# x loaded first, gate exponentials by polynomial, first expert weights rounded between blocks, and one 512-column tile in each turn of the selection

## The chip, the cores and the metric

The kernel runs on one core of a Trainium2 chip. The metric is the device time of one execution in microseconds (us). The kernel before took 918.75 us, the median of 3 runs (917.81 to 918.88).

## The reference

One layer of a hybrid model: 256 tokens, width 1024, all in float32. Three mixers (a state-space scan, block attention of 8 heads, retention of 4 heads) share one input projection; their outputs are normalised, projected and added to x. Then comes an expert layer, which takes most of the time:

```python
def peer_layer(h, w_q, sub_keys, u_emb, v_emb):
    q = (hf @ w_q).reshape(t, PEER_HEADS, 2, PEER_QDIM // 2)
    sc = jnp.einsum('thcd,hcnd->thcn', q, sub_keys)
    sv, si = lax.top_k(sc, PEER_TOPK)
    cand_s = (sv[:, :, 0, :, None] + sv[:, :, 1, None, :]).reshape(...)
    cand_i = (si[:, :, 0, :, None] * PEER_KEYS + si[:, :, 1, None, :]).reshape(...)
    fs, fp = lax.top_k(cand_s, PEER_TOPK)
    eidx = jnp.take_along_axis(cand_i, fp, axis=-1)
    gates = jax.nn.softmax(fs, axis=-1)
    ...
        act = jax.nn.gelu(jnp.einsum('cd,chkd->chk', xc, u_emb[ic]))
        return jnp.einsum('chk,chkd->cd', gc * act, v_emb[ic])
```

There are 16384 experts. Each token uses 8 x 16 of them.

## The kernel before, in words

**Precision by halves.** Every float32 product of the projections and of the expert layer is made of three matmuls of rounded operands: high x high, high x low, low x high (`halves_product`, lines 439 to 441). ScalarE (ACT) rounds a slice of weights into `w_hi`, GpSimd (POOL) subtracts to give `w_lo`, TensorE (PE) multiplies. For the values the subtraction is VectorE's (DVE).

**The expert layer is dense.** All 16384 experts are multiplied, in 128 tiles of 128 (`NT`), four tiles to a turn (`UN` = 4), 32 turns (`TURNS`). In the first pass (`keys_turn`) a tile of u is multiplied with h for all 256 tokens, passed through Gelu by ACT (line 1603) and kept in memory outside the chip (`spill`). A selection of each token's experts runs beside it on DVE. From turn `G_TURN0` = 15 the selection becomes a dense matrix of gates (`one_hots`, `group_out`). In the second pass (`values_turn`) activations times gates are multiplied with the tiles of v. Tiles of u stand in one of two PSUM banks, 0 or 1, by `s % 2`, so PE starts tile s of a turn only once the Gelu of tile s - 2 is done (`act_ready`, line 727).

**Wide tiles.** A tile whose s is in `wide` is made otherwise (lines 738 to 747): `w_hi` is multiplied in one matmul of 512 columns with `h_both`, the high and the low half of h side by side, so the product with the low half lies in columns 256 to 511 of the bank. ACT copies that part to `low_out` (line 1618, increments `part_ready`), DVE adds it into the first part (`add_part`, increments `added`), and only then does ACT make the Gelu. A tile has then 16 matmuls instead of 24. Before, turns 0, 1, 12, 13 and 14 have three wide tiles each (`WIDE_TURNS`), the turns from 15 on two; turns 2 to 11 have none.

**The order of each engine is written by hand**, and each engine works its list in order. ACT, for each tile of a turn (line 1605 on): the rounding of the next tile in two halves (`high`, lines 1590 to 1597), what is `extra`, the Gelu of a wide tile before this one (it waits for `added`), then the low part's copy or the Gelu of this tile. POOL: two subtractions for each tile (line 1717). The DVE list between the adds of turn 1 and those of turn 12 is the selection: for each half of the tokens (t = 0, 1) `best` over 16 rows of 128 key scores (lines 1185 to 1199: eight best of each row, their indices and a copy without them, the next eight, their indices), sums of pairs in `w2`, `best` over 8 rows of 256 sums, differences to the best one (line 1231), and for both halves of a pair an index look-up by comparison, product and reduction (lines 1240 to 1242). `step` and `settle` wait until DVE's own results are there.

**Gates.** After the selection DVE reports (`diff_ready`), ACT takes the exponentials in turn 13 (`gate_exps`, line 1642), DVE divides by the sums and reports (`tok_ready`, line 1252), and PE transposes the rows before turn 14.

**Queries and the first tile.** The 16 slices of w_q are multiplied in two rounds of 8 (line 690 on): the first round fills banks 4 to 7, the second banks 0 to 3. ACT copies four query banks to `pqT` in `queries(n)` (line 1571). During the second round h is scaled: DVE multiplies into banks 5 to 7, ACT rounds to `h_hi` (line 1583), DVE subtracts to `h_lo`. Then ACT rounds the first expert tile (`high(0, 0, 0)`), runs `queries(1)`, waits for DVE's copy of iota into bank 2 (line 1207) and starts turn 0.

**Beginning and end.** SyncE's queue (SP) issues the loads in this order: parameters, identity, rotations, x in two halves, first weights, constants, and so on (lines 337 to 362). PE is kept at work by 9 matmuls until x is there. At the end DVE adds the four result tiles (two column halves, two token halves) to x; it waits for `half_used`, which counts column halves.

Of the kernel before, what the change touches and what calls it, by code (L numbers as in the profile page):

```python
# [19 lines left out]
F32 = mybir.dt.float32  # L20
F32R = mybir.dt.float32r
U32 = mybir.dt.uint32
ALU = mybir.AluOpType
# [37 lines left out]
OUT_BANKS = ((2, 6), (0, 1))  # L61
ROW_BANKS = (2, 3, 0, 1)
# [11 lines left out]
WIDE_TURNS = {0: 0, 1: 3, EXP_TURN - 1: 6, EXP_TURN: 9, ROUTE_TURN: 12}  # L74
WIDE_S, WIDE_G_S, WIDE_G0 = (0, 1, 2), (0, 2), 15
# [46 lines left out]
def build(nc, x, w_in, vecs, consts, rots, decay, mask, s5_b, s5_c, w_glu, w_out, w_q, keys, u_t, v, out, spill):  # L122
    with ExitStack() as ctx:
# [150 lines left out]
        diff_ready, gate_exp = sem("gate_exponents_ready"), sem("gate_exp_ready")  # L274
# [5 lines left out]
        sum_ready, stored = sem("sum_ready"), sem("stored")  # L280
# [55 lines left out]
        def _(sp):  # L336
            sp.dma_start(vec[:], vecs).then_inc(params_in, 16)
            sp.dma_start(ident, consts[:, C_ID:C_ID + P]).then_inc(con_in, 16)
            sp.dma_start(rawf[:, 256:256 + ROPE_N], rots[:, 0:ROPE_N]).then_inc(rope_in, 16)
# [3 lines left out]
            sp.dma_start(w_ring[0][:, 0:4, 0:S5_CH], first[:, 0:4]).then_inc(first_in, 16)  # L343
            sp.dma_start(times, consts[:, C_IOTA:C_N]).then_inc(times_in, 16)
            sp.dma_start(w_ring[0][:, 4:KC, 0:S5_CH], first[:, 4:KC]).then_inc(w_in_sem[0], 16)
# [63 lines left out]
        def _(pe):  # L409
# [36 lines left out]
            keep_warm(mv[:, 0, 0:P], 7, 9)  # L446
# [241 lines left out]
            for n in range(2):  # L688
                for k in range(KC):
# [6 lines left out]
                    for h in range(4):  # L696
                        c = slice(h * P, (h + 1) * P)
                        mm = halves_product(ps[:, 4 * (1 - n) + h, 0:S],
# [6 lines left out]
                    if n == 1 and k == 2:  # L705
                        pe.wait_ge(rows_ready, 1)
                        pe.wait_ge(pq_ready, 4)
                        for t in range(TT):
                            mm = pe.matmul(ps[:, 4, t * P:(t + 1) * P], rstd_rows[:, t, :], ident, start=True, stop=True)
# [50 lines left out]
            pe.wait_ge(keys_in, 16)  # L760
            key_scores(0)
# [3 lines left out]
            with pe.Fori(2, EXP_TURN - 1) as t:  # L765
                keys_turn(t)
# [16 lines left out]
            def values_turn(t, first=False, last=False):  # L783

                for s in range(UN):
                    pe.wait_ge(w_ready, UN * t + s + 1)
                    for h in range(2):
# [7 lines left out]
                        mm.then_inc(half_used, 1)  # L795
# [8 lines left out]
        def _(dve):  # L804
# [370 lines left out]
            for k in range(KC + 2):  # L1175
                if k >= 2:
                    dve.wait_ge(th_ready, 3 * KC + k - 1)
                    tt(h_lo[:, H2_PLACE[k - 2], :], ps[:, 5 + (k - 2) % 3, 0:S], h_hi[:, H2_PLACE[k - 2], :].bitcast(F32),
                       ALU.subtract).then_inc(tl_ready, 1)
                if k < KC:  # L1180
                    if k >= 3:
                        dve.wait_ge(tl_ready, 3 * KC + k - 2)
                    tt(ps[:, 5 + k % 3, 0:S], hT[:, k, :], ps[:, 4, 0:S], ALU.mult).then_inc(scaled_ready, 1)

            def best(dst, where, src, scratch):
# [604 lines left out]
```

## Time and profile before

| what | value |
|---|---|
| profiled execution, own time | 918.49 us |
| its span, first to last instruction | 916.7 us |
| median of 3 runs | 918.75 us |
| PE busy, share of the span | 903.1 us, 99% |
| DVE, ACT, POOL busy | 713.8, 557.2, 424.9 us |
| mean granted clock of PE | 0.998 of full speed |
| chain that ended last: PE, ACT, DVE, POOL | 93%, 4%, 1%, 1% |
| all waits of PE for POOL's L1717, for ACT's L1603 | 2.5 us (1), 1.4 us (2) |
| ACT table loads | 10, of 1.28 us |

How to read it: PE is busy nearly all the time, and a matmul's record is longer than the distance to the next one (they overlap), so a PE that is busy is not yet one that could not be faster. The distance between the starts of its matmuls tells more. The span is cut in stages: mixers and projections to about 110 us, output projection and queries to 157, turns 0 and 1 to 188.6, turns 2 to 11 with the selection to 303.8, turns 12 to 14 to about 340, the rest of the first pass to about 562, the second pass to 913.

### The profile page before, as it was taken

Reading aid. Unit: us, or ns where it says so; the run is one execution under the profiler, and the core shown is the slowest. Engines: PE = TensorE matmul, PEld = TensorE weight load, DVE = VectorE, ACT = ScalarE, POOL = GpSimd, SP = SyncE. Lnnn points to the kernel's source line nnn. Section 1 sums busy time; section 2 is a strip of 40 time slices with the busy share of each in tenths; the row PEclk is TensorE's granted clock in tenths of the full one; section 3 lists DMA queues with packets and bytes.
Section 4 is the critical chain, followed back from the end, with each engine's and each line's share of the span. In section 5 each row is a group of like instructions: output and inputs, shape, how many; then the busy total and the mean of one; then the engine's idle time right before and its main releaser. Section 6 shows DMA issues by size and latency. Waiting matters only on the chain.

```text
span 916.7 us, 19407 instructions
## 1 busy us (share of the span) xinstructions
PE 903.1 (99%) x5480; PEld 798.9 (87%) x5480; DVE 713.8 (78%) x1604; ACT 557.2 (61%) x1113; POOL 424.9 (46%) x340
## 2 busy tenths in 40 slices
PE   8999998999999999999999999999999999999998
PEld 6877888899999989999999999888888888888886
DVE  6989533099997138898988986888888888888886
ACT  7658565555555666666666666565665656556563
POOL 4874386788888887777777774000000000000000
PEclk9999999999999999999999999999999999999999
DMA  9824050466666666655656566777777677777773
GB/s 327 297 102 181 3 207 1 161 223 224 229 227 228 230 213 205 196 201 187 204 193 197 194 206 210 256 234 242 248 236 245 231 246 244 242 239 233 249 241 124
DMA packets 67756, 191.54 MB, mean 209 GB/s; under 512 B 6672, under 2 KB 8592, under 8 KB 67728
## 3 DMA queue, kind: packets, MB, share of 16 engines
q1 hardware_dynamic: 67728, 191.19, 61.9%
q8 instruction: 15, 0.25, 0.1%
q14 instruction: 13, 0.11, 0.0%
HBM read 173.86 MB, written 17.30 MB: 209 GB/s over the span
## 4 chain that ended last, share of the span: by engine, by line
PE 93%; ACT 4%; DVE 1%; issue 1%; POOL 1%; DMA 0%; SPq 0%; DVEq 0%; POOLq 0%; ACTq 0%
PE ps L439 24%; PE ps L441 24%; PE ps L440 24%; PE ps L744 9%; PE ps L746 4%; PE ps L754 3%; ACT routing L1432 1%; PE ps L743 1%; ACT w_hi L1363 1%; DMA xs<-in_x 0%; POOL w_lo L1702 0%; PE ps L717 0%; PE ps L595 0%; PE ps L431 0%; DVE routing L813 0%
## 5 line engine op out<-in xcount | busy, mean ns | idle before, releaser
L1596 ACT ACTIVATE w_hi<-raw 128x512 fp32r<-128x512 f32 x512 | 308.3, 628 | 134.1 <-PE ps L441 130.4
L1717 POOL TENSOR_TENSOR w_lo<-raw,w_hi 128x512 fp32r<-128x512 f32 x256 | 326.9, 1298 | 80.9 <-ACT w_hi L1596 80.4
L813 DVE TENSOR_TENSOR w_lo<-raw,w_hi 128x512 fp32r<-128x512 f32 x256 | 177.4, 693 | 52.8 <-ACT w_hi L1596 41.4
L439 PE MATMUL ps<-h_both,w_hi 128*128 128x256 f32 x712 | 201.9, 284 | 0.0
L441 PE MATMUL ps<-h_both,w_lo 128*128 128x256 f32 x712 | 201.5, 283 | 0.0
L440 PE MATMUL ps<-h_both,w_hi 128*128 128x256 f32 x712 | 201.4, 283 | 0.0
L439 PE MATMUL ps<-w_hi,hot_gate 128*128 128x512 f32 x512 | 199.2, 389 | 0.0
L440 PE MATMUL ps<-w_lo,hot_gate 128*128 128x512 f32 x512 | 199.2, 389 | 0.0
L441 PE MATMUL ps<-w_hi,hot_gate 128*128 128x512 f32 x512 | 199.2, 389 | 0.0
L744 PE MATMUL ps<-h_both,w_hi 128*128 128x512 f32 x376 | 137.5, 403 | 3.9 <-POOL w_lo L1717 2.5
L439 PEld LDWEIGHTS ps<-h_both,w_hi 128*128 128x128 f32 x712 | 136.0, 191 | 0.4 <-POOL w_lo L1702 0.2
L440 PEld LDWEIGHTS ps<-h_both,w_hi 128*128 128x128 f32 x712 | 136.0, 191 | 0.2
L441 PEld LDWEIGHTS ps<-h_both,w_lo 128*128 128x128 f32 x712 | 136.0, 191 | 0.0
L441 PEld LDWEIGHTS ps<-w_hi,hot_gate 128*128 128x128 f32 x512 | 96.1, 188 | 20.0
L440 PEld LDWEIGHTS ps<-w_lo,hot_gate 128*128 128x128 f32 x512 | 96.1, 188 | 20.0
L439 PEld LDWEIGHTS ps<-w_hi,hot_gate 128*128 128x128 f32 x512 | 96.1, 188 | 19.8
L1702 POOL TENSOR_TENSOR w_lo<-routing,w_hi 128x512 fp32r<-128x512 f32 x72 | 92.3, 1299 | 45.2 <-ACT w_hi L1363 43.6
L1603 ACT ACTIVATE acts<-ps 128x256 f32<-128x256 f32 x128 | 49.1, 383 | 100.8 <-PE ps L441 93.7
L1281 DVE SCALAR_TENSOR_TENSOR hot_gate<-ps,route_t 128x256 fp32r<-128x256 f32 x256 | 105.7, 476 | 0.0
L746 PE MATMUL ps<-h_both,w_lo 128*128 128x256 f32 x329 | 93.0, 283 | 0.0
L744 PEld LDWEIGHTS ps<-h_both,w_hi 128*128 128x128 f32 x376 | 70.9, 190 | 18.1 <-ACT routing L1574 2.7
L813 DVE TENSOR_TENSOR route_t<-acts,routing 128x256 f32<-128x256 f32 x128 | 81.7, 638 | 4.3 <-ACT acts L1603 2.1
(222 smaller groups left out, 1109.7 us busy)
## 6 DMA issues: line engine op xcount, KB each, us to landing
raw<-in_u_t SPq DMA_DIRECT2D x128, 512.0 KB, 3.4
raw<-in_v SPq DMA_DIRECT2D x128, 512.0 KB, 3.3
act_spill<-acts SPq DMA_DIRECT2D x62, 256.0 KB, 2.2
acts<-act_spill SPq DMA_DIRECT2D x62, 256.0 KB, 3.4
routing<-in_w_in SPq DMA_DIRECT2D x4, 2048.0 KB, 12.8
routing<-in_w_out SPq DMA_DIRECT2D x2, 2048.0 KB, 8.2
routing<-in_w_q SPq DMA_DIRECT2D x2, 2048.0 KB, 7.6
routing<-in_w_in SPq DMA_DIRECT2D x2, 1024.0 KB, 9.6
```

Source lines behind the costliest of these rows:

```text
L439: pe.matmul(dst, s_hi, m_hi, start=first and i == 0, stop=False)
L440: pe.matmul(dst, s_hi, m_lo, start=False, stop=False)
L441: mm = pe.matmul(dst, s_lo, m_hi, start=False, stop=end)
L744: mm = pe.matmul(ps[:, s % 2, :], s_hi, both, start=(h == 0 and k == 0), stop=end)
L746: mm = pe.matmul(ps[:, s % 2, 0:S], s_lo, m_hi, start=False, stop=False)
L754: mm = pe.matmul(ps[:, 4 + 2 * (s % 2) + q // 2, (q % 2) * 2 * NKEY:(q % 2 + 1) * 2 * NKEY], hot_j[:, s % 2, q, :], hot_gate[:, s % 2, q]. ...
L813: return V.tensor_tensor(out_, a, b, op)
L1281: ins = V.scalar_tensor_tensor(hot_gate[:, s % 2, q], iota_p.unsqueeze(1).to_broadcast([P, 2, NKEY]), route_t[:, 0, one], route_t[:, 2:4, ...
L1596: A.activation(w_hi[:, 2 * (s % 2) + h, :], raw[:, s, h * HALF:(h + 1) * HALF], ACT.Copy)\
L1603: A.activation(acts[:, s, :], ps[:, s % 2, 0:S], ACT.Gelu_apprx_tanh).then_inc(act_ready, 1)
L1702: G.tensor_tensor(w_lo[:, m % 4, :], w_ring[n % W_SLOTS][:, k, :], w_hi[:, m % 4, :].bitcast(F32), ALU.subtract).then_inc(lo_ready, 1)
L1717: G.tensor_tensor(w_lo[:, slot, :], raw[:, s, h * HALF:(h + 1) * HALF], w_hi[:, slot, :].bitcast(F32), ALU.subtract).then_inc(lo_ready, 1)
```

## The change

It does the following.

- The loads of identity, `vec` and rotations are issued from ACT's queue, in that order, before ACT's first square; SP starts with x, and the second part of the first weights goes ahead of the constants. Seven matmuls instead of nine keep PE at work. On ACT the copies `full(0)` and `full(1)` stand before the first exponential, `full(2)` and `full(3)` before the square root.
- A Gelu of one element is put behind the square root of the third norm.
- The banks of both query rounds, of the rows' transposes, of the output projection's second half and of the scaled h are exchanged (0 to 3 for 4 to 7). The first expert tile's two roundings are put behind blocks 4 and 5 of the scaled h; `queries(1)` is put into tile 0 of turn 0, behind the rounding of tile 1; DVE copies iota as soon as its last `h_lo` is written; PE starts turn 0 when all blocks are scaled.
- In turns 2 to 11 (`WIDE_PICK_S` = (0,), `N_PICK` = 10) the first tile of each turn is wide. DVE makes the ten adds at five places in each half of the selection.
- The gates' exponentials are computed by DVE, by the polynomial of eight terms that the kernel uses for another exponential, and the adds of turn 12 are put between its steps.
- At the end PE reports each of the four result tiles by itself (`out_psum`).

```diff
-OUT_BANKS = ((2, 6), (0, 1))
-ROW_BANKS = (2, 3, 0, 1)
+OUT_BANKS = ((2, 6), (4, 5))
+ROW_BANKS = (6, 7, 4, 5)
...
-WIDE_TURNS = {0: 0, 1: 3, EXP_TURN - 1: 6, EXP_TURN: 9, ROUTE_TURN: 12}
-WIDE_S, WIDE_G_S, WIDE_G0 = (0, 1, 2), (0, 2), 15
+WIDE_PICK_S = (0,)
+N_PICK = EXP_TURN - 3
+WIDE_TURNS = {0: 0, 1: 3, EXP_TURN - 1: 6 + N_PICK, EXP_TURN: 9 + N_PICK, ROUTE_TURN: 12 + N_PICK}
+WIDE_S, WIDE_G_S, WIDE_G0 = (0, 1, 2), (0, 2), 15 + N_PICK
...
         def _(sp):
-            sp.dma_start(vec[:], vecs).then_inc(params_in, 16)
-            sp.dma_start(ident, consts[:, C_ID:C_ID + P]).then_inc(con_in, 16)
-            sp.dma_start(rawf[:, 256:256 + ROPE_N], rots[:, 0:ROPE_N]).then_inc(rope_in, 16)
             for t in range(TT):
...
-            keep_warm(mv[:, 0, 0:P], 7, 9)
+            keep_warm(mv[:, 0, 0:P], 7, 7)
...
             def keys_turn(t, groups=None, first=False, first_group=False, wide=()):
                 for s in range(UN):
-                    if first and s < 2:
-                        pe.wait_ge(pq_ready, 4 + s + 1)
-                    else:
+                    if first and s == 0:
+                        pe.wait_ge(scaled_ready, KC)
+                    elif not (first and s < 2):
                         pe.wait_ge(act_ready, UN * t + s - 1)
...
             with pe.Fori(2, EXP_TURN - 1) as t:
-                keys_turn(t)
+                keys_turn(t, wide=WIDE_PICK_S)
...
+                            if last and s == UN - 1:
+                                mm.then_inc(out_psum, 1)
+                        if not (last and s == UN - 1):
+                            mm.then_inc(half_used, 1)
...
-            dve.wait_ge(pq_ready, PH)
+            dve.wait_ge(tl_ready, 4 * KC)
             V.tensor_copy(iota_p, iota).then_inc(iota_ready, 1)
...
             def best(dst, where, src, scratch, first=None, second=None):
                 for d_, s_ in zip(dst, src):
                     did(V.max(d_[:, 0:8], s_))
                 settle()
+                if first is not None:
+                    add_part(first, 0)
                 for d_, w_, s_, x_ in zip(dst, where, src, scratch):
                     did(V.max_index(w_[:, 0:8], d_[:, 0:8], s_))
                     did(V.match_replace(x_, d_[:, 0:8], s_, LOWEST))
                 settle()
                 for d_, x_ in zip(dst, scratch):
                     did(V.max(d_[:, 8:16], x_))
                 settle()
+                if second is not None:
+                    add_part(second, 0)
...
-                     [sc[:, t, c, h, :] for c, h in ch_rows], [work[:, c, h, :] for c, h in ch_rows])
+                     [sc[:, t, c, h, :] for c, h in ch_rows], [work[:, c, h, :] for c, h in ch_rows], 6 + 5 * t, 7 + 5 * t)
...
-                     [work3[:, h * 256:(h + 1) * 256] for h in range(PH)])
+                     [work3[:, h * 256:(h + 1) * 256] for h in range(PH)], 8 + 5 * t)
+                add_part(9 + 5 * t, 0)
...
                     step(tt(w3, match_p, idx_f[:, c].unsqueeze(2).to_broadcast(shape), ALU.mult))
+                    if c:
+                        add_part(10 + 5 * t, 0)
                     step(V.tensor_reduce(rows[:, t, c, :].rearrange("p (h k) -> p h k", h=PH), w3, AX.X, ALU.add))
-            V.tensor_copy(top2[:, 0, 0:1], top2[:, 0, 1:2]).then_inc(diff_ready, 1)
-            add_parts(EXP_TURN - 1)
-            dve.wait_ge(gate_exp, TT)
...
+            step(V.tensor_scalar(rest_g, gates, -150.0, None, ALU.max))
+            step(V.tensor_scalar(turns_g, rest_g, float(1 / np.log(2)), ROUND, ALU.mult, ALU.add))
+            step(V.tensor_scalar(turns_g, turns_g, -ROUND, None, ALU.add))
+            for ln2_part in (LN2_1, LN2_2):
+                step(V.scalar_tensor_tensor(rest_g, turns_g, -ln2_part, rest_g, ALU.mult, ALU.add))
+            add_part(WIDE_TURNS[EXP_TURN - 1], 0)
+            step(V.tensor_scalar(turns_g, turns_g, -127.0, 127.0, ALU.max, ALU.min))
+            did(V.tensor_scalar(power_g.bitcast(mybir.dt.int32), turns_g, 127.0, float(2 ** 23), ALU.add, ALU.mult))
+            step(V.tensor_scalar(sum_g, rest_g, EXP_C[0], None, ALU.mult))
+            for c_ in EXP_C[1:3]:
+                step(V.scalar_tensor_tensor(sum_g, sum_g, c_, rest_g, ALU.add, ALU.mult))
+            add_part(WIDE_TURNS[EXP_TURN - 1] + 1, 1)
+            for c_ in EXP_C[3:]:
+                step(V.scalar_tensor_tensor(sum_g, sum_g, c_, rest_g, ALU.add, ALU.mult))
+            add_part(WIDE_TURNS[EXP_TURN - 1] + 2, 2)
+            step(V.scalar_tensor_tensor(gates, sum_g, 1.0, power_g, ALU.add, ALU.mult))
...
             for h in range(2):
-                dve.wait_ge(half_used, TAIL + 4 * NT - 1 + h)
                 for t in range(TT):
+                    dve.wait_ge(out_psum, TT * h + t + 1)
...
+            act.dma_start(ident, consts[:, C_ID:C_ID + P]).then_inc(con_in, 16)
+            act.dma_start(vec[:], vecs).then_inc(params_in, 16)
+            act.dma_start(rawf[:, 256:256 + ROPE_N], rots[:, 0:ROPE_N]).then_inc(rope_in, 16)
             squares_x(0)
+            act.wait_ge(params_in, 16)
+            full(0)
+            full(1)
             act.wait_ge(expo_ready, 1)
...
             root(ss_x, 0, 1.0 / D)
+            A.activation(spare, quarter, ACT.Gelu_apprx_tanh)
             slices_high(range(FRONT + 21, FRONT + 3 * KC))
...
+                if k in (4, 5):
+                    high(0, 0, 0, (k - 4,))
...
-            high(0, 0, 0)
-            queries(1)
             act.wait_ge(iota_ready, 1)
-            wide_turn(0, first=True)
+            def last_queries(s):
+                if s == 0:
+                    queries(1)
+
+            wide_turn(0, first=True, extra=last_queries)
...
-            with act.Fori(3, EXP_TURN - 1) as t:
-                keys_turn(t)
+            with act.Fori(3, EXP_TURN - 1) as t:
+                keys_turn(t, wide=WIDE_PICK_S, wide_0=t + 4)
```

## Rows read from the trace of the kernel before

**Rows 1.** Windows: stretch, length, busy time and instructions of each engine, PEclk granted

```profile
160.40:162.50 2.10, 2.10 (x8) 1.80 (x7) 0.00 (x0) 0.69 (x2) 2.00 (x3) 0.51 0.35 84
...
188.60:303.80 115.20, 115.20 (x960) 115.20 (x961) 103.64 (x397) 58.85 (x121) 100.46 (x80) 1.00 0.68 224
```

**Rows 2.** Timeline of PE around turn 0: start, us, [idle before, releaser]

```profile
156.70 0.28 PE L441 MATMUL ps<-h_both,w_lo 128*128 128x256 f32 x1
159.47 0.77 PE L744 MATMUL ps<-h_both,w_hi 128*128 128x512 f32 x1 [2.49 <-POOL w_lo L1717]
...
167.10 0.50 PE L744 MATMUL ps<-h_both,w_hi 128*128 128x512 f32 x1 [0.39 <-ACT acts L1603]
```

**Rows 3.** Timelines of POOL, ACT and DVE around turn 0

```profile
151.05 3.81 POOL L1702 TENSOR_TENSOR w_lo<-routing,w_hi 128x512 fp32r<-128x512 f32 x3 [2.67 <-ACT w_hi L1363]
158.05 5.12 POOL L1717 TENSOR_TENSOR w_lo<-raw,w_hi 128x512 fp32r<-128x512 f32 x4 [3.19 <-ACT w_hi L1596]
...
157.35 1.14 ACT L1596 ACTIVATE w_hi<-raw 128x512 fp32r<-128x512 f32 x2
158.39 1.19 ACT L1574 ACTIVATE routing<-ps 128x256 f32<-128x256 f32 x4
...
165.37 1.28 ACT L1603 ACT_TABLE_LOAD   x1
...
157.49 0.42 DVE L813 TENSOR_TENSOR h_both<-ps,h_both 128x256 fp32r<-128x256 f32 x1 [1.01 <-ACT h_both L1583]
159.62 0.29 DVE L1207 COPY ps<-con 128x128 f32<-128x128 f32 x1 [1.71 <-ACT routing L1574]
```

**Rows 4.** Timelines of ACT, DVE and PE in turns 12 and 13

```profile
306.85 0.39 ACT L1618 ACTIVATE con<-ps 128x256 f32<-128x256 f32 x1 [1.41 <-PE ps L744]
...
309.63 0.38 ACT L1618 ACTIVATE con<-ps 128x256 f32<-128x256 f32 x1 [1.09 <-PE ps L744]
...
307.26 0.43 DVE L813 TENSOR_TENSOR ps<-ps,con 128x256 f32<-128x256 f32 x1 [13.79 <-ACT con L1618]
...
321.04 0.42 DVE L813 TENSOR_TENSOR ps<-ps,con 128x256 f32<-128x256 f32 x1
...
320.50 0.40 PE L744 MATMUL ps<-h_both,w_hi 128*128 128x512 f32 x1
321.93 0.50 PE L744 MATMUL ps<-h_both,w_hi 128*128 128x512 f32 x1 [1.03 <-ACT acts L1603]
```

**Rows 5.** Timelines of POOL and PE in the first query round

```profile
137.03 2.54 POOL L1702 TENSOR_TENSOR w_lo<-routing,w_hi 128x512 fp32r<-128x512 f32 x2 [0.44 <-ACT w_hi L1363]
...
134.41 0.36 PE L439 MATMUL ps<-h_both,w_hi 128*128 128x256 f32 x1
```

**Rows 6.** Timeline of DVE: first instruction behind each place of an add, tokens' first half

```profile
189.00 0.09 DVE L1191 MATCH_VALUE_LOAD routing<-routing 128x8 f32 x1
...
200.71 0.09 DVE L1198 MATCH_VALUE_LOAD routing<-routing 128x8 f32 x1
...
210.91 0.09 DVE L1191 MATCH_VALUE_LOAD routing<-routing 128x8 f32 x1
...
223.40 0.74 DVE L813 TENSOR_TENSOR routing<-routing 128x128 f32<-128x128 f32 x1
...
236.41 2.29 DVE L1242 TENSOR_REDUCE routing<-routing 128x128 f32<-128x2048 f32 x1
```

**Rows 7.** Timeline of DVE: one line of the selection, first and second half

```profile
224.06 0.22 DVE L1234 TENSOR_SCALAR routing<-routing 128x128 uint32<-128x128 uint32 x1
...
277.56 1.31 DVE L1234 TENSOR_SCALAR routing<-routing 128x128 uint32<-128x128 uint32 x1
```

**Rows 8.** Timelines of SP's queue, DVE and PE in the beginning

```profile
2.13 0.91 SPq L341 DMA_DIRECT2D xs<-in_x  x2
...
2.73 0.17 DVE L835 TENSOR_SCALAR small<-vec 128x8 f32<-128x8 f32 x1 [1.70 <-DMA vec<-in_vecs]
...
17.45 0.66 PE L512 MATMUL ps<-con,raw 128*128 128x128 f32 x4 [0.99 <-ACT raw L1464]
```

**Rows 9.** Timeline of DVE at the end

```profile
911.49 2.64 DVE L813 TENSOR_TENSOR xs<-xs,ps 128x512 f32<-128x512 f32 x4 [2.72 <-PE ps L441]
```

More of the change, by code:

```diff
@@ L1182, in _, with add_part, best @@
                         dve.wait_ge(tl_ready, 3 * KC + k - 2)
-                    tt(ps[:, 5 + k % 3, 0:S], hT[:, k, :], ps[:, 4, 0:S], ALU.mult).then_inc(scaled_ready, 1)
-            def best(dst, where, src, scratch):
+                    tt(ps[:, 1 + k % 3, 0:S], hT[:, k, :], ps[:, 0, 0:S], ALU.mult).then_inc(scaled_ready, 1)
+            ch_rows = [(c, h) for c in range(2) for h in range(PH)]
+            shape = [P, PH, PK, PK]
+            w2 = work2.rearrange("p (h a b) -> p h a b", h=PH, a=PK)
+            w3 = work3.rearrange("p (h a b) -> p h a b", h=PH, a=PK)
+            iota_k = iota_p[:, 0:PK].unsqueeze(1).unsqueeze(1).to_broadcast(shape)
+            dve.wait_ge(tl_ready, 4 * KC)
+            V.tensor_copy(iota_p, iota).then_inc(iota_ready, 1)
+            dve.wait_ge(iota_ready, 1)
+            def add_part(n, s):
+                dve.wait_ge(part_ready, n + 1)
+                tt(ps[:, s % 2, 0:S], ps[:, s % 2, 0:S], low_out, ALU.add).then_inc(added, 1)
+            def best(dst, where, src, scratch, first=None, second=None):
                 for d_, s_ in zip(dst, src):
@@ L1247, in _ @@
-            step(V.tensor_reduce(gsum, gates, AX.X, ALU.add))
+            gates = rows[:, :, 2, :]
+            by_t = lambda a: a.rearrange("p (t n) -> p t n", t=TT)
+            rest_g, power_g = by_t(work2[:, 0:2 * P]), by_t(work2[:, 2 * P:4 * P])
+            turns_g, sum_g = by_t(ps[:, 4, 0:2 * P]), by_t(ps[:, 5, 0:2 * P])
+            settle()
+            step(V.tensor_scalar(rest_g, gates, -150.0, None, ALU.max))
+            step(V.tensor_scalar(turns_g, rest_g, float(1 / np.log(2)), ROUND, ALU.mult, ALU.add))
@@ L1446, in _ @@
             squares_x(1)
-            full(0)
-            full(1)
+            full(2)
+            full(3)
             act.wait_ge(zeros_ready, 4)
@@ L1568, in _, with high @@
             root(ss_x, 0, 1.0 / D)
+            A.activation(spare, quarter, ACT.Gelu_apprx_tanh)
             slices_high(range(FRONT + 21, FRONT + 3 * KC))
+            def high(n, s, turn, halves=(0, 1)):
+                act.wait_ge(raw_in[s], 16 * turn + 16)
+                for h in halves:
+                    act.wait_ge(half_used, TAIL + 2 * n + h - 3)
+                    A.activation(w_hi[:, 2 * (s % 2) + h, :], raw[:, s, h * HALF:(h + 1) * HALF], ACT.Copy)\
+                        .then_inc(hi_ready, 1)
             def queries(n):
@@ L1589, in key_scores @@
                              scale=rstd[:, t:t + 1]).then_inc(sc_ready, 1)
-            def high(n, s, turn, halves=(0, 1)):
-                act.wait_ge(raw_in[s], 16 * turn + 16)
-                for h in halves:
-                    act.wait_ge(half_used, TAIL + 2 * n + h - 3)
-                    A.activation(w_hi[:, 2 * (s % 2) + h, :], raw[:, s, h * HALF:(h + 1) * HALF], ACT.Copy)\
-                        .then_inc(hi_ready, 1)
             def gelu(t, s, first):
```

49 lines of the change are left out of this document (16 added, 33 removed).

## The prediction

> **What bounds the kernel now.** I read the busy table first, then the windows, then the timeline of TensorE (PE) wherever its starts are not evenly spaced, then the engine that releases it. In the first turns and the selection PE decides: in the 115.20 us of turns 2 to 11 it issued 960 matmuls without a gap, 0.120 us apart, 24 to a tile, 2.88 us a tile [rows 1]. A change pays there only by fewer PE cycles or by removing a PE wait. The reader should see three such waits. (1) Before the first expert tile: the last query matmul starts at 156.70 and the first expert one at 159.47, released by POOL, and behind it the granted clock is 0.51, the lower level (1.2 GHz), for a stretch [rows 1, 2]. (2) Turn 0, tile 2, at 167.10, behind an ACT table load [rows 2, 3]. (3) Turn 13, tile 2, at 321.93, behind another [rows 4].
>
> **The parts, each priced.** The profiled execution took 918.49 us, 1.79 more than its span of 916.70, and 0.26 less than the median, 918.75. The sum is made against 918.49.
>
> *First expert weights, banks.* Now ACT rounds them at 157.35, after the last of its eight h_hi copies, and POOL's first low half starts at 158.05 although its slices ended at 154.86 (151.05 + 3.81) [rows 3]. After: the two roundings stand behind copies 4 and 5, whose semaphore values they share, so half 0 is rounded by about 153.8 and POOL does its halves at 154.9 and 156.2, 1.27 each. PE starts tile 0 at 156.82, its second half at 158.2; the last low part of h ends at 157.91 (157.49 + 0.42) [rows 3], in time. The wait and the slow clock go. Late next is tile 1: ACT may round it only after the copy of iota, which moves from 159.62 to about 157.97; ACT follows some 0.33 later, POOL 0.70 after ACT starts (157.35 to 158.05) with 1.27, PE 0.15 (159.32 to 159.47 [rows 2]): 160.42, where PE wants it at 156.82 + 2.80 = 159.62. Tile 1 then ends at about 163.3. queries(1), 1.19 of ACT [rows 3], now lies in tile 0, and tile 2's rounding ends at 162.0, its low half at 162.9: covered. The Gelu table (1.28, 165.37 [rows 3]) is loaded early, so tile 2 starts at 163.3 instead of 167.10: **-3.8**. If tile 1 took no wait it would be -4.6; if POOL slipped another tile half, -2.5.
>
> *The early table load* costs ACT about 1.5 in the query stage. POOL's next slice starts at 137.03 and ends 1.3 later; PE's query slices start at 134.41 and last 12 x 0.12 = 1.44, so that slice (the fifth after this start) is wanted at 140.17 [rows 5]. 1.5 later is 139.8: hidden by 0.4, **0**; without this cover up to +1.1.
>
> *Exponentials.* The ACT pair in turn 13 goes. PE's starts were 320.50 and 321.93, 1.43 apart where 0.23 is usual, and the matmuls behind a wait lose 0.1 more [rows 4]: **-1.3**. The 16 polynomial steps of 256 columns are bounded by the 256-column add, 0.43 [rows 4]. They are taken between the adds of turn 12, five at a time: 5 x 0.43 + 0.43 = 2.6 < 2.8. The rest ends soon after turn 12's third tile, and all of turn 13, over 11 us, lies before the route transposes that wait for it: **0**.
>
> *Wide tiles.* ACT's copies of two such tiles are 2.78 apart [rows 4]; I take 2.815, since a tile alone has normal ones on both sides, against 2.88: 10 tiles x 0.065 = **-0.65** (-0.4 to -1.0). The ten extra copies on ACT (0.39 [rows 4]) stand in its idle time before a tile ends.
>
> *What the ten adds wait for* is the new term. Each is written into DVE's selection at a fixed place, five in each half. The part is ready once a turn, every 4 x 2.88 - 0.065 = 11.455. In a turn that goes well DVE's add starts 0.41 behind ACT's copy, and PE's matmul of two tiles on starts 0.89 behind the add [rows 4] (321.93 - 321.04). PE wants that tile 2.88 - 0.21 = 2.67 behind the copy (turn 12 starts at 303.80 [rows 1], its first tile ends 2.82 later and is copied at 306.85, some 0.2 behind); so an add may be 2.67 - 0.41 - 0.89 = 1.37 late for nothing, and beyond it PE waits. DVE's own work between the places, start to start [rows 6]: 11.71 (189.00 to 200.71), 10.20 (to 210.91), 12.49 (to 223.40), 13.01 (to 236.41); then 5.55 in the next half. An add puts 0.34 to it. The first add is on time: DVE is there at 189.00, and turn 2 starts at 188.60 [rows 1], so that its first tile ends at 191.4. Then:
> second add 11.71 + 0.34 - 11.455 = 0.6 late, no wait; third 0.6 + 0.34 + 10.20 - 11.455 < 0, on time; fourth 12.49 + 0.34 - 11.455 = 1.38 late, no wait; fifth 1.38 + 0.34 + 13.01 - 11.455 = 3.27 late.
> To this comes what DVE loses beside POOL: the same 128x128 shift took 0.22 at 224.06 and 1.31 at 277.56 [rows 7], there across one of POOL's 1.27 instructions. With the adds in, the segment begins 2.13 behind a copy, and POOL's pair runs from 0.98 (0.28 for the copy, 0.70) to 3.53, which puts the shift behind its second half as at 277.56: 0.6 more than in the first half of before, 3.9 late. PE waits 3.9 - 1.37 = 2.5, with 0.1 for the restart 2.6. This comes at turn 6, tile 2, and, the second half being alike, at turn 11, tile 2. **+5.2**, bounds 2 x 2.0 = +4.0 (no collision) and 2 x 3.4 = +6.8 (both operations collide). Below: 0, if adds were never late, which needs the 13.01 to shrink by 2.
> The Trainium skill (GPSIMD Engine Reference, Specifications) says that POOL's SBUF interface is shared with VectorE and contended by instructions in a two-port mode or with two SBUF inputs. The trace agrees (1.31 against 0.22). It speaks against the change here, since the added wait makes such steps fall at other moments.
>
> *Start.* x is issued 1.38 earlier (2.13 to 0.75), but vec is now second on ACT's queue and DVE's chain, which starts on it at 2.73, is later by an issue (0.42) or more; PE waits at 17.45 for ACT, where two copies move from behind the second square to before it [rows 8]. No row prices the new order; between -1.4 (the whole shift) and +0.5 (vec's delay on the path), and both ends as near, the middle: **-0.5**. Two warm-up matmuls less: PE waits for x anyway, 0.
>
> *End.* DVE's four last adds, 2.64 together [rows 9], were released by halves; now by tiles of three matmuls, so that one add (0.66) instead of two is left behind the last matmul: **-0.6** (0 to -0.7).
>
> Sum: -3.8 - 1.3 - 0.65 + 5.2 - 0.5 - 0.6 = -1.65, or 918.49 - 1.65 = 916.8; I say **916.9**, 0.20% below the median, on the edge of what a measurement tells from no change (0.2%, 1.8 us, so 916.9 to 920.6 counts as the same).
>
> **Rivals.**
> - *The adds are in time or nearly so.* For: per half DVE has 52.96 + 5 x 0.34 = 54.7 of work for 57.3, so only the places are wrong, not the load; should a step be quicker, the lateness shrinks one for one. Against: the step times above are alike in both halves. No waits: 916.9 - 5.2 = 911.7; one wait of 2.6: 914.3. Chance 0.22.
> - *The clock falls in a wait.* PE idle for 2.49 before 159.47 [rows 2] was followed by a stretch at 0.51, where 8 matmuls took 2.10 [rows 1] and 16 fill 2.8 otherwise. The two new waits are as long. Some 3 us at half speed (159.47 to 162.50) lose about 1.5. One fall 918.4, two 919.9. For: equal idle time. Against: PE was busy right up to both. Chance 0.23. The Trainium skill (TensorE: Matmul & The Clock Gate, Why this matters for your kernels) says to leave no long idle gap between bursts of matmuls, or the engine returns to the lower clock; the row at 0.51 agrees.
> - *The other side: DVE collides with POOL at both steps of the segment and the clock falls each time.* Place: tile 2 of turns 6 and 11. Price: 6.8 instead of 5.2, and 2 x 1.5: 916.9 + 1.6 + 3.0 = 921.5. It decides once the fifth add is over 4.5 late, so that PE idles for over 3. Chance 0.06.
> - *The early rounding does not take effect* (POOL or ACT in another order), and the first wait stays: 916.9 + 3.8 = 920.7. Chance 0.03. Against: the semaphore values are reached in the trace before ACT would ask.
>
> **How the numbers follow.** Forecast 0.46, its own range 915.5 to 918.6 by the collision bounds and the start. Below 916.9 lie half of it (0.24) and the first rival (0.22): faster 0.46. Slower: the third rival and part of the fourth, 0.07. The same: 0.47. For 8 in 10 the range takes in one missing wait and both clock falls: 913.6 to 919.9.
>
> **What would show it.** First expert matmul within 0.3 of the last query one; clock 1.00 there; tile 2 of turn 0 some 3.8 earlier. No table load on ACT between turn 0 and the end. Turns 2 to 11: waits of PE on ACT's Gelu, only in tile 2 of turns 6 and 11, 2.0 to 3.4 each, with the DVE add late behind its copy by as much more than 0.41. If PE waits in other turns, or nowhere, the segment sum is wrong; if the granted clock is below 1.00 after them, the second rival has come. Last DVE adds: one behind the last matmul.

## The result and the profile after

| | kernel before | kernel after |
|---|---|---|
| median | 918.59 us (4 runs) | 926.70 us (4 runs, 925.41 to 928.30) |
| ratio | | 1.0097 (95% interval 1.0085 to 1.0110) |
| profiled execution, span | 918.49, 916.7 us | 928.30, 926.4 us |
| PE's mean granted clock, share of full speed | 0.998 | 0.992 |

The change makes the kernel 8.1 us slower, where 916.9 was forecast. The ratio is not the quotient of the two medians, which is 1.0088. The profiled execution of after is the slowest of its four; the two spans differ by 9.7.

The timeline of after: selected instructions from four stretches, the start, the first expert tile, the selection and the end. Others that lie between them are left out. In brackets stand the idle time ahead and what ended it:

```profile
0.74 0.42 ACTq L1470 DMA_DIRECT2D con<-in_consts  x1
1.19 0.46 ACTq L1471 DMA_DIRECT2D vec<-in_vecs  x1
4.89 1.09 PE L414 MATMUL ps<-con,xs 128*128 128x128 f32 x8 [0.47 <-DMA con<-in_consts]
6.75 0.17 DVE L837 TENSOR_SCALAR small<-vec 128x8 f32<-128x8 f32 x1 [5.72 <-DMA vec<-in_vecs]
9.99 0.21 ACT L1478 ACTIVATE small<-small 128x8 f32<-128x8 f32 x1 [2.05 <-DVE small L815]
10.10 1.04 ACT L1407 ACTIVATE routing<-xs 128x1024 f32<-128x1024 f32 x1
19.56 0.66 PE L510 MATMUL ps<-con,raw 128*128 128x128 f32 x4 [2.35 <-ACT raw L1495]
...
161.14 0.28 PE L439 MATMUL ps<-h_both,w_lo 128*128 128x256 f32 x1
161.26 0.40 PE L742 MATMUL ps<-h_both,w_hi 128*128 128x512 f32 x1
...
228.32 0.43 DVE L815 TENSOR_TENSOR ps<-ps,con 128x256 f32<-128x256 f32 x1
228.87 1.31 DVE L1241 TENSOR_SCALAR routing<-routing 128x128 uint32<-128x128 uint32 x1
230.33 2.59 POOL L1747 TENSOR_TENSOR w_lo<-raw,w_hi 128x512 fp32r<-128x512 f32 x2 [0.24 <-ACT w_hi L1608]
230.35 1.43 DVE L1244 CAST routing<-routing 128x256 f32<-128x256 uint32 x1
238.18 0.38 ACT L1652 ACTIVATE con<-ps 128x256 f32<-128x256 f32 x1 [1.25 <-PE ps L742]
243.44 0.43 DVE L815 TENSOR_TENSOR ps<-ps,con 128x256 f32<-128x256 f32 x1
308.15 0.53 PE L437 MATMUL ps<-h_both,w_hi 128*128 128x256 f32 x1 [3.41 <-ACT acts L1637]
...
921.20 2.73 DVE L815 TENSOR_TENSOR xs<-xs,ps 128x512 f32<-128x512 f32 x4 [2.04 <-PE ps L439]
922.82 0.39 PE L439 MATMUL ps<-w_hi,hot_gate 128*128 128x512 f32 x1
```

Turn 0 went as forecast: the first expert matmul, 161.26, stands 0.12 behind the last query one, where PE had waited 2.49 [rows 2]. The start did not: DVE begins at 6.75 instead of 2.73 and PE at 19.56 instead of 17.45 [rows 8]. In the selection the fifth add of the first half is at 243.44, its copy at 238.18; PE then waits 3.41 in each half (its next matmuls are at 244.42 and 308.15).

The windows of after; the columns are length, PE's busy time (matmuls), its granted clock, DMA share and GB/s:

```profile
19.50:23.00 3.50, 3.14 (x13) 0.79 1.08 376
23.00:27.00 4.00, 4.00 (x19) 0.76 1.03 388
156.00:190.00 34.00, 33.41 (x256) 1.00 0.47 156
244.40:247.80 3.40, 3.38 (x16) 0.50 0.64 196
247.80:251.20 3.40, 3.40 (x21) 0.65 0.61 189
308.10:311.60 3.50, 3.45 (x16) 0.52 0.61 211
311.60:315.00 3.40, 3.40 (x30) 0.99 0.53 169
```

Turn 0 now runs at full clock, against 0.51 in [rows 1]; but the clock falls at three places: in the start, and behind each of the two waits (0.50 is the lower level, 1.2 GHz).

Where the 9.7 us of span came from, by PE's starts in the two profiles (first matmul of the same place, before and after):

| stretch | before | after | difference |
|---|---|---|---|
| up to the transposes of the first normalised rows | 124.20 | 128.36 | +4.16 |
| from there up to the query slice of [rows 5] | 134.41 | 138.84 | +0.27 |
| from there up to turn 2 | 188.49 | 188.98 | -3.94 |
| turns 2 to 11 | 115.33 long | 126.52 long | +11.19 |
| turns 12 and 13, up to the route transposes | 23.91 long | 22.60 long | -1.31 |
| all up to the last matmul | 584.69 long | 584.72 long | 0.0 |
| behind the last matmul | 4.28 long | 3.58 long | -0.7 |

Two rows stand far from their terms: the start (+4.4 against -0.5) and turns 2 to 11 (+11.2 against 5.2 - 0.65 = +4.5).

### The profile page after: what moved, and what is told of

Read it like the earlier page. It is cut to its first block, busy times and chain, and to the rows that moved or that the text cites. A ratio compares the mean times of both kernels' runs of the same rounds, so it can differ in the third digit from the quotient of the medians.

```text
span 926.4 us, 19297 instructions
## 1 busy us (share of the span) xinstructions
PE 906.9 (98%) x5396; PEld 797.9 (86%) x5396; DVE 724.3 (78%) x1629; ACT 554.8 (60%) x1120; POOL 425.6 (46%) x340
## 4 chain that ended last, share of the span: by engine, by line
PE 87%; DVE 7%; ACT 3%; POOL 1%; issue 1%; DMA 1%; ACTq 0%; POOLq 0%; DVEq 0%
PE ps L437 22%; PE ps L439 21%; PE ps L438 21%; PE ps L742 11%; PE ps L744 5%; PE ps L752 3%; DVE ps L815 1%; DVE routing L815 1%; ACT routing L1459 1%; DVE routing L1218 1%; DVE routing L1210 1%; DVE routing L1209 1%; PE ps L741 1%; POOL w_lo L1732 1%; DMA vec<-in_vecs 1%
## 5 line engine op out<-in xcount | busy, mean ns | idle before, releaser
L437 PE MATMUL ps<-h_both,w_hi 128*128 128x256 f32 x632 | 181.5, 287 | 6.9 <-ACT acts L1637 6.8
L438 PE MATMUL ps<-h_both,w_hi 128*128 128x256 f32 x632 | 180.6, 286 | 0.0
L742 PE MATMUL ps<-h_both,w_hi 128*128 128x512 f32 x456 | 165.0, 399 | 0.6 <-POOL w_lo L1747 0.6
L437 PEld LDWEIGHTS ps<-h_both,w_hi 128*128 128x128 f32 x632 | 122.4, 194 | 8.0 <-issue 7.6
L438 PEld LDWEIGHTS ps<-h_both,w_hi 128*128 128x128 f32 x632 | 122.4, 194 | 0.3
L439 PEld LDWEIGHTS ps<-h_both,w_lo 128*128 128x128 f32 x632 | 122.4, 194 | 0.0
L742 PEld LDWEIGHTS ps<-h_both,w_hi 128*128 128x128 f32 x456 | 85.3, 188 | 17.0 <-POOL w_lo L1747 0.9
```

The source lines that it names most:

```text
L437: pe.matmul(dst, s_hi, m_hi, start=first and i == 0, stop=False)
L438: pe.matmul(dst, s_hi, m_lo, start=False, stop=False)
L439: mm = pe.matmul(dst, s_lo, m_hi, start=False, stop=end)
L742: mm = pe.matmul(ps[:, s % 2, :], s_hi, both, start=(h == 0 and k == 0), stop=end)
```

## Experiments

Each kernel was run in several rounds beside the kernel before, whose median was 918.5 to 918.6 in each set; the ratios are against that. The kernel after (926.70) was not run again in these sets, so a difference against it compares runs of different sets. Experiments 1 to 7 and 9 have a short diff; the others are described.

**1. Without the ten wide tiles.** On the kernel after:

```
-WIDE_PICK_S = (0,)
+WIDE_PICK_S = ()
-N_PICK = EXP_TURN - 3
+N_PICK = 0
```
and the ten `add_part` calls of the selection are left out.

> Edit: the changed kernel without its ten wide tiles in turns 2 to 11 (all tiles of these turns as before the change) and without their ten adds. Theory A (the fifth add of each half is 4.85 us behind its part's copy, PE waits 3.57 in each half, and the clock falls in each wait): turns 2 to 11 fall from 126.5 to 115.3 us, no PE wait there, granted clock 1.00 throughout, so about 917.1 against the changed kernel's profiled 928.3. Rival A1 (the lower clock in these turns has another cause than the waits): only the 7.1 of the waits goes and a low clock stays somewhere in these turns, about 921.8 (928.3 - 7.1 + 0.65). Whatever is left above the kernel before comes from the start: about +4.4 at PE's first landmarks.

Measured: 916.47 us (0.9976 of before, 0.9967 to 0.9985). No wait of PE is left in turns 2 to 11, the clock is 1.00 there, and they take 115.32 us (115.33 before the change). The whole +11.2 belongs to the ten tiles, the low clock included.

**2. The fifth add two steps earlier.** On the kernel after:

```
                 for c in range(2):
+                    if c:
+                        add_part(10 + 5 * t, 0)
                     step(tt(match_p, ...))
                     step(tt(w3, match_p, ...))
-                    if c:
-                        add_part(10 + 5 * t, 0)
                     step(V.tensor_reduce(...))
```

> Edit: the fifth add of each half stands two DVE steps (4.6 us) earlier, ahead of the second comparison. Theory A (only its place is wrong, DVE's load is not: 54.7 us of work for 57.3): no add is over 1.4 late, no PE wait in turns 2 to 11, granted clock 1.00 there, these turns take 114.7 (115.33 less 10 x 0.065), so about 928.3 - 11.8 = 916.5. Rival A2 (DVE has too much to do beside the adds, so that lateness only moves to another add): PE still waits some 7 us in all, in other turns, and the time stays within 2 us of 928. Rival A1 (low clock without the waits): about 921.

Measured: 916.36 us (0.9973, 0.9963 to 0.9984), as theory A had it. No load was taken away, one line moved, and 10.3 us came back: only the place was wrong. Theory A2, too much work on DVE, falls.

**3. The fifth add one step earlier**, between comparison and product.

> Edit: the fifth add stands one DVE step (2.3 us) earlier, between the second comparison and its product. Theory A: it is 4.85 - 2.3 = 2.55 late, PE waits 2.55 - 1.37 = 1.2 and 0.1 for the restart in tile 2 of turns 6 and 11, 2.6 in all against 7.1: 928.3 - 4.5 = 923.8 if the clock falls in these shorter waits as it did in the longer ones, 919.1 if it does not. Rival A2 (no slack on DVE): waits of over 3 us in all. What it tells apart beside this: whether the clock falls at a wait of 1.2 us.

Measured: 918.32 us (0.9997, 0.9988 to 1.0006). The timeline of this kernel, ACT's copy, DVE's add and PE's two waits:

```profile
238.20 0.38 ACT L1652 ACTIVATE con<-ps 128x256 f32<-128x256 f32 x1 [1.25 <-PE ps L742]
241.12 0.43 DVE L815 TENSOR_TENSOR ps<-ps,con 128x256 f32<-128x256 f32 x1
242.10 0.38 PE L437 MATMUL ps<-h_both,w_hi 128*128 128x256 f32 x1 [1.06 <-ACT acts L1637]
300.98 0.38 PE L437 MATMUL ps<-h_both,w_hi 128*128 128x256 f32 x1 [1.07 <-ACT acts L1637]
```

The add is 2.92 - 0.41 = 2.5 late; the start of PE's matmul comes 1.35 behind the one before, so the wait costs 1.23. The allowance of 1.37 holds, and beyond it PE waits one for one (2.5 - 1.37 = 1.1, and 0.1 for the restart). Its windows behind the waits:

```profile
242.00:245.50 3.50, 3.40 (x28) 1.00 0.63 185
300.90:304.00 3.10, 3.02 (x25) 1.00 0.54 189
```

A wait of 1.06 leaves the clock at 1.00; the clock falls behind the 3.41 of the kernel after. So the last 2.3 us of lateness of each half cost 8.4 us together (926.7 - 918.3): 4.7 of waiting, and the rest, 3.7, is put down to the clock.

**4. The start as before.** On the kernel after: the vectors, identity and rotations again first on SP, the constants again ahead of the second part of the first weights, ACT's old order, nine warm-up matmuls. The banks stay exchanged.

> Edit: the changed kernel with the start of the kernel before (the vectors, the identity and the rotations issued first on SyncE, ACT's old order of the first squares, copies and the exponential, nine warm-up matmuls). Theory B (the changed start costs 4.2 us since the vectors land 4 us later, with the first DVE chain behind them): PE's first driven states end at 22.3 instead of 26.55, every later landmark up to the end of the front part is 4.2 earlier, about 928.3 - 4.2 = 924.1. Rival B1 (the loss of the front part comes from something else, the banks or the clock): under 1 us earlier, above 927. The two waits in the selection stay (turns 2 to 11 about 126 us).

Measured: 922.36 us (1.0039, 1.0027 to 1.0051), 4.3 less than after. The transposes stand at 124.34 (before 124.20), and the +0.27 behind them is gone too, so the exchange of banks, which this kernel keeps, costs nothing. PE's waits in the selection stay at 3.40. Theory B holds for the sum; the next three runs split it.

**5. The vectors first on SP**, all else of the new start kept:

```
+            sp.dma_start(vec[:], vecs).then_inc(params_in, 16)
             for t in range(TT):
                 sp.dma_start(xs[:, t, :], ...).then_inc(x_in[t], 16)
...
-            act.dma_start(vec[:], vecs).then_inc(params_in, 16)
```

> Edit: the changed kernel with one DMA moved: the vectors are issued first on SyncE's queue, ahead of x, and no longer second on ACT's; everything else of the new start stays (identity and rotations on ACT, ACT's new order, seven warm-up matmuls). Theory B (only the late landing of the vectors costs): they land some 2.0 us after an issue at 0.75, DVE's chain starts at about 2.8 instead of 6.75, ACT's exponential does not wait for DVE, and PE's wait at 19.56 comes 3.5 to 4.5 us earlier, so 922.2 to 923.2 against the changed kernel's 926.7. Rival B2 (ACT's new order costs for itself, since the exponential and the second square stand behind copies that wait for PE): 1 to 2 us stay, 924 to 925.

Measured: 924.91 us (1.0070, 1.0056 to 1.0083). Only 1.8 of the 4.3 comes back: theory B in this form falls, and theory B2 (924 to 925) holds. Timeline of this kernel:

```profile
2.94 0.17 DVE L838 TENSOR_SCALAR small<-vec 128x8 f32<-128x8 f32 x1 [1.91 <-DMA vec<-in_vecs]
8.14 0.84 ACT L1430 ACTIVATE routing<-ps,vec 128x256 f32<-128x256 f32 x2 [2.07 <-PE ps L415]
8.97 1.05 ACT L1408 ACTIVATE routing<-xs 128x1024 f32<-128x1024 f32 x1
18.45 0.66 PE L511 MATMUL ps<-con,raw 128*128 128x128 f32 x4 [2.12 <-ACT raw L1495]
126.66 1.03 PE L667 MATMUL ps<-con,xs 128*128 128x128 f32 x8
```

DVE is as early as before the change, and still ACT idles 2.07 ahead of its first copies, which wait for PE's transposes. The second square, whose half of x is there by 7.60 (PE's second transposes start on it then), stands behind them and starts at 8.97.

**6. The vectors first on ACT's queue**, ahead of the identity.

> Edit: the changed kernel with the vectors and the identity exchanged on ACT's queue, the vectors first. Theory B (the vectors share the DMA engines with x and the first weights, issued in the same microseconds on the other queue): issued 0.45 us earlier they still need 4 to 5.5 us, so DVE starts at 5 to 6.3 instead of 6.75, a gain of 0.5 to 1.8: 925 to 926.3. Rival B3 (they are late because they are served behind the identity on ACT's queue): they land in some 2.5 us, DVE starts at 3.3, and nearly the whole 4.2 comes back, about 922.8, unless the identity, now late, holds PE's first transposes.

Measured: 925.54 us (1.0075, 1.0062 to 1.0088), inside theory B's range. The profiled execution is the fastest of the five, 920.97; the others took 923.47 to 925.86. Its wait of PE in the start is 1.29 (at 18.27), with the clock at 1.00 behind it. Issues and landing of this kernel (KB, us from issue to landing):

```profile
vec<-in_vecs ACTq DMA_DIRECT2D x1, 89.0 KB, 4.1
con<-in_consts ACTq DMA_DIRECT2D x1, 64.0 KB, 5.2
```

And of the kernel after, where they are issued the other way round:

```profile
vec<-in_vecs ACTq DMA_DIRECT2D x1, 89.0 KB, 5.5
con<-in_consts ACTq DMA_DIRECT2D x1, 64.0 KB, 4.1
```

Whichever is issued at 0.75, beside the first half of x on SP's queue, takes 4.1; the next takes over 5. With the identity late, PE's transposes start at 6.43 instead of 4.89. In experiment 5, where the vectors were issued beside the identity and x 0.45 later, the identity took 2.4 from ACT's queue. So ACT's queue is not slow in itself, and rival B3 (the vectors are late because they stand behind the identity) falls: first on that queue they still take 4.1. What fits all three is that the small loads share the DMA engines with 1 MB of x and the first weights. The Trainium skill (DMA: Bandwidth & Descriptors, Issuing engines are not separate DMA queues) says the same: DMAs issued by different engines run on the same 16 and interleave, and only time of issue is saved.

**7. The kernel before with ACT's new order alone.**

```
             squares_x(0)
+            act.wait_ge(params_in, 16)
+            full(0)
+            full(1)
             act.wait_ge(expo_ready, 1)
             A.activation(mag, expo, ACT.Exp).then_inc(mag_ready, 1)
             squares_x(1)
-            full(0)
-            full(1)
+            full(2)
+            full(3)
```
(and `full(2)`, `full(3)` no longer behind the root).

> Edit: the kernel before with nothing changed but the order of ACT's first instructions (copies 0 and 1 ahead of the exponential and the second square, as in the changed kernel); all DMAs as before. Theory B2 (the order costs for itself where x is not early): ACT is idle for about 1.3 us behind its first square, until PE's transposes end, and its square root and the rounded copies come 1.3 later: +1.3, 919.9. Rival B (the order is free, only the landing counts): 918.6 within 0.3.

Measured: 920.22 us (1.0015, 1.0005 to 1.0025), near theory B2's 919.9. Timeline of this kernel:

```profile
7.93 0.84 ACT L1402 ACTIVATE routing<-ps,vec 128x256 f32<-128x256 f32 x2 [0.79 <-PE ps L416]
8.75 1.06 ACT L1380 ACTIVATE routing<-xs 128x1024 f32<-128x1024 f32 x1
18.23 1.00 PE L512 MATMUL ps<-con,raw 128*128 128x128 f32 x4 [2.17 <-ACT raw L1465]
126.45 1.03 PE L668 MATMUL ps<-con,xs 128*128 128x128 f32 x8
```

The second half of x is there by 7.39, but the second square starts at 8.75. The direct delay at PE is 18.23 - 17.45 = 0.78; at the transposes it is 2.25 (126.45 - 124.20). Between the two lies a window at the lower clock, behind a wait of 2.17 where before had 0.99:

```profile
18.00:22.00 4.00, 3.77 (x13) 0.57 1.05 382
22.00:26.00 4.00, 4.00 (x23) 1.00 1.06 384
```

The runs without a trace say the same. Three of the twelve have a mean clock of 1.000 and took 917.37 to 918.05, beside 916.95 to 917.60 for the five such runs of the kernel before in this set; the other nine took 918.88 to 921.37, beside 918.24 to 919.17. So the order costs little by itself, and most of its price is clock.

**8. Both costs taken out**: the kernel of experiment 2 with the start of experiment 4.

> Edit: the changed kernel with both costs taken out: the start of the kernel before and the fifth add two DVE steps earlier; the rest of the change (early rounding, banks, polynomial, ten wide tiles, stepwise last adds) stays. If theories A and B name the whole loss and the two add up: 926.7 - 4.3 - 10.3 = 912.1, that is 6.5 under the kernel before, by the terms -3.9 (turn 0), -1.3 (exponentials), -0.65 (wide tiles) and -0.7 (end). If the parts hang together (a start 4.3 earlier meets other collisions of DVE with POOL in the selection), above 914.

Measured: **912.60 us** (912.25 to 912.95; 0.9938, 0.9925 to 0.9951), 14.1 under the kernel after and 6.0 under the kernel before. It beats both, and its mean clock is 1.000. The two costs add up.

**9. The fourth add earlier too.**

```
-    [work3[:, h * 256:(h + 1) * 256] for h in range(PH)], 8 + 5 * t)
-add_part(9 + 5 * t, 0)
+    [work3[:, h * 256:(h + 1) * 256] for h in range(PH)], 8 + 5 * t, 9 + 5 * t)
```

> Edit: the last kernel (start of before, fifth add two steps earlier) with the fourth add of each half moved ahead of the last eight index searches of the pairs, some 3.1 us earlier. In that kernel the fourth add is still 1.44 us behind its part and the turn that uses it takes 11.70 us from copy to copy where the others take 11.46. Theory A: it is then on time, all turns take 11.46, two times 0.24 go, 912.6 - 0.5 = 912.1, and turns 2 to 11 take 114.7. Rival A3 (the 0.24 is not from the add but from the loop or from DVE's collision with POOL in the segment behind it): one turn in each half still takes 11.70, 912.6 within 0.2. The median alone can hardly tell; the distances of ACT's copies can.

Measured: 913.93 us (0.9951, 0.9938 to 0.9963): a miss, 1.3 slower than experiment 8. Timeline of this kernel:

```profile
223.25 0.43 DVE L818 TENSOR_TENSOR ps<-ps,con 128x256 f32<-128x256 f32 x1 [1.97 <-ACT con L1650]
234.22 0.38 ACT L1650 ACTIVATE con<-ps 128x256 f32<-128x256 f32 x1 [1.25 <-PE ps L745]
236.77 0.43 DVE L818 TENSOR_TENSOR ps<-ps,con 128x256 f32<-128x256 f32 x1
237.75 0.38 PE L440 MATMUL ps<-h_both,w_hi 128*128 128x256 f32 x1 [0.69 <-POOL w_lo L1745]
```

The fourth add is on time, indeed too early: DVE stands still 1.97 for it. The eight index searches it was moved past now lie between it and the fifth, 13.52 of work in a turn of 11.46, and the fifth is 2.1 late again. PE's record names POOL, whose second half of this tile ends just then, but PE asks for the first half first, and that was done 1.3 earlier; what it had to wait for is the Gelu, which ACT could only start at 237.23, 0.46 behind the add. Theory A was right about the 0.24 (all other turns take 11.46 now), but its sum for the next segment was not made. Each half wins 0.24 and loses 0.94 (12.40 from copy to copy), 1.4 in all, which is the 1.3. The profiled execution alone, 914.59, is also late in the start (PE's first transposes 0.8 later than in experiment 8).

**10 to 12. The other parts, each alone on the kernel before.** Experiment 10: the turn 0 part (early rounding, banks, early Gelu table). Experiment 11: the gates' exponentials by polynomial. Experiment 12: the four last adds released tile by tile.

> Edit: the kernel before with only the turn 0 part: the first expert weights rounded behind copies 4 and 5, the banks exchanged, the early Gelu table, the second queries' copies inside tile 0, the copy of iota behind the last low part. Start, exponentials, tiles of turns 2 to 11 and last adds as before. The forecast term: -3.8 (the two traces gave -3.94), so 918.6 - 3.9 = 914.7. Rival C (part of the -3.94 belongs to the changed phase behind the slow start): 915.5 or more.

Measured: 914.58 us (0.9963, 0.9950 to 0.9976), -3.9 as forecast.

> Edit: the kernel before with only the exponentials by polynomial on DVE between the adds of turn 12, and without ACT's pair of exponentials. Forecast term: PE's wait in tile 2 of turn 13 goes, -1.3, 917.3. Rival D (the 16 DVE steps delay the adds of turn 12 or the rows for the route transposes): a new PE wait in turns 12 to 14, 918 or more.

Measured: 917.16 us (0.9987, 0.9977 to 0.9997), -1.4. No PE wait is left in turns 12 to 14.

> Edit: the kernel before with only the four last adds released tile by tile. Forecast term: one add instead of two behind the last matmul, -0.6 to -0.7: 918.0. Rival E (the last store sets the end, its landing as long as before, and hides it): 918.6.

Measured: 916.83 us (0.9987, 0.9978 to 0.9996), -1.7. Behind the last matmul the profile shows 915.0 - 911.37 = 3.63 against 4.28, so -0.65 as forecast. The rest of the -1.7 is luck of the clock: 8 of its 12 runs have a mean clock of 1.000, against 8 of 23 of the kernel before. Among the runs at 1.000 the medians are 916.8 and 917.2, among the others 918.1 and 918.9, so 0.4 to 0.8 is the edit's. In the profiled execution the clock did not fall in turn 0 behind the same wait. The window there in this kernel:

```profile
159.70:162.70 3.00, 2.98 (x17) 1.00 0.22 52
```

against the one in the kernel of experiment 11:

```profile
159.90:162.90 3.00, 2.94 (x11) 0.64 0.21 48
```

## Why the prediction was wrong, point by point

The profiled execution took 928.3 where the sum gave 916.8. Of these 11.5 us the start has 4.9, and turns 2 to 11 have 6.6: 1.9 of longer waits, 0.5 behind the fourth adds, and 4.2 of clock.

**First expert weights, early table load, banks: right.** -3.8 forecast, -3.94 in the profiles, -3.9 alone (experiment 10). Tile 1 waited for POOL as worked out (it started 3.55 behind tile 0, at 164.81; 3.60 was forecast), the table load was hidden.

**Exponentials: right.** -1.3 forecast, -1.31 and -1.4.

**End: right.** -0.6 forecast, -0.65 to -0.7.

**Wide tiles: mis-sized.** "10 tiles x 0.065 = -0.65". The turns with a tile take 11.46 from copy to copy as forecast, but the one behind the fourth add takes 11.70 in each half: that add is 1.43 late where 1.37 were allowed, so PE just waits. Experiment 9, with that add on time, has 11.46 there. -0.65 + 0.48 = -0.2; experiments 1 and 2, without and with the ten tiles, differ by 0.1.

**What the ten adds wait for: the mechanism right, the size short.** Two waits, at tile 2 of turns 6 and 11, with the third rival's double collision in both. The failed step here is "which puts the shift behind its second half as at 277.56: 0.6 more", that is, one collision. After it DVE's cast fell on POOL's next pair: 1.43 at 230.35, where in the kernel before it took 0.29. The fifth add was 5.26 - 0.41 = 4.85 late, not 3.9, and PE's matmul came 3.69 behind the one before: 3.57 a wait, 7.1 in all against 5.2. The upper bound of 2 x 3.4, "both operations collide", had the right mechanism and was 0.3 short. What decides between one collision and two is smaller than the profile can resolve. In experiment 6 the cast is recorded 0.01 behind POOL's pair and took 0.29, in the kernel after 0.02 behind and took 1.43; in experiment 8 both outcomes stand in one execution, at the same 0.01. The lines of experiment 6:

```profile
227.82 2.70 POOL L1747 TENSOR_TENSOR w_lo<-raw,w_hi 128x512 fp32r<-128x512 f32 x2 [0.25 <-ACT w_hi L1608]
227.83 0.29 DVE L1244 CAST routing<-routing 128x256 f32<-128x256 uint32 x1
240.77 0.38 PE L437 MATMUL ps<-h_both,w_hi 128*128 128x256 f32 x1 [2.27 <-ACT acts L1637]
```

And those of experiment 8, first and second half:

```profile
225.98 2.59 POOL L1746 TENSOR_TENSOR w_lo<-raw,w_hi 128x512 fp32r<-128x512 f32 x2 [0.24 <-ACT w_hi L1607]
225.99 1.43 DVE L1247 CAST routing<-routing 128x256 f32<-128x256 uint32 x1
...
283.49 2.70 POOL L1746 TENSOR_TENSOR w_lo<-raw,w_hi 128x512 fp32r<-128x512 f32 x2 [0.25 <-ACT w_hi L1607]
283.50 0.29 DVE L1247 CAST routing<-routing 128x256 f32<-128x256 uint32 x1
```

Where the cast took 0.29, POOL's pair took 2.70 instead of 2.59. In experiment 6 this was so in both halves, and PE waited 2.27 and 2.28: with one collision the forecast of 2.5 would have held. The Trainium skill (SBUF — State Buffer, Who interferes with whom) says that whoever issues first holds the shared ports for its whole instruction and the other is blocked; the rows agree in that one of the two pays each time (1.43 beside 2.59, or 0.29 beside 2.70); who issued first they cannot show. So an execution can go either way. Whether that is why the kernel of experiment 6 gave 920.97 once and 923.5 to 925.9 in its other runs is not shown, since only the first has a trace.

**The clock in the waits: given too little.** The second rival had 0.23 and the third 0.06 for a fall; it fell in both, once for a double stretch. Turns 2 to 11 are 11.19 longer: 7.14 for the waits, 0.48 for the fourth adds, -0.65 for the tiles, and the remaining 4.2 is clock: the turn from the fifth copy to the next takes 17.65 and 16.61 us, so 2.6 and 1.6 beyond 11.46 and the wait of 3.57. The reason against it, "PE was busy right up to both", was no reason: PE had been busy up to the wait of [rows 2] too. Experiment 3 shows the link from the other side, since shorter waits at the same places leave the clock at 1.00.

**The start: the failed step.** "No row prices the new order; between -1.4 (the whole shift) and +0.5 (vec's delay on the path), and both ends as near, the middle: -0.5". Measured +4.3, outside both ends. Three things were left out. (a) The landing: 2.0 became 5.5. "Later by an issue (0.42) or more" put a number on the issue alone, and not on x and the weights, which now share the DMA engines with it. Experiment 5 prices it with all that hangs on it: 1.8. (b) ACT's order: the copies wait for PE's transposes, and ready work (the second square, then the root) stands behind them; directly 0.78 at PE (experiment 7). (c) The clock: a wait of PE of 0.99 [rows 8] became 2.12 to 2.35 (1.29 only in the profiled execution of experiment 6), and the clock fell behind it, about 1.5 of the 2.25 in experiment 7. At the transposes experiment 5 takes back 1.70 and experiment 7 alone costs 2.25, together 3.95 of the 4.16; by the medians 1.8 + 1.6 = 3.4 of the 4.3. The rest can lie in the warm-up matmuls, the order of the first weights and the identity, which were not tested one by one. Not run either is x first with the vectors ahead of it and ACT's old order, so whether the earlier x is worth anything stays open. The row at 0.51 behind 2.49 [rows 1, 2] was already there to price (c).

By the medians the account closes: 918.6 - 3.9 - 1.3 - 0.65 - 0.2 = 912.5 is experiment 8 (912.6), and 912.6 + 4.3 + 10.3 = 927.2, the kernel after (926.7).

## What to carry to other kernels

Where extra work is written at fixed places into another engine's list, sum the list from place to place against the period of the producer, and give every place the collisions it can meet at the worst, since the sum in between counts and not the load; then move the place, one line, before dropping the idea. A large load issued beside small ones can delay these (here from 2.0 to 5.5 us), and an instruction moved ahead in an engine's list delays all that was ready behind it: price both by the wait of the engine that follows. A PE wait as long as those measured here (2.1 us and more) is to be priced with a likely clock fall on top (some 1.5 us each), and removing one is worth that much more, and steadier runs.

## What was not expected of the hardware

The clock after a PE wait is partly chance. Behind the same wait of turn 0 (2.48 to 2.49) it was 0.51 [rows 1] and 0.64 (experiment 11), and 1.00 in experiment 12; in experiment 6 a wait of 2.27 left it at 1.00 and one of 2.28 brought 0.54. Behind the waits of 3.40 and more it fell each time (six of six, in the kernel after and experiments 4 and 5), behind those of 1.06 and 1.07 never. It shows without a trace too: of 17 runs of the kernel before beside experiments 5 to 8, five have a mean clock of 1.000 and took 916.95 to 917.60, the others 918.24 to 919.17. The kernels of experiments 8 and 9, without a wait of PE over 1.0 behind the first 15 us, spread by 0.7 and 0.9 us; with two long ones the spread is wide (experiment 4: 919.15 to 924.14).

At the lower clock the matmuls of 256 columns started 0.21 to 0.22 apart (0.12 otherwise), less than twice; a stretch of 3.4 us so costs 1.5.

Whether a DVE cast of 0.29 takes 1.43 cannot be told from the recorded starts: at 0.01 us behind POOL's start the traces have both. So two executions of one program can differ by over 1 us a wait.
